# Second maxima and probabilities moved ahead of the output sum and its squares in a hybrid block's steady step

## The reference

```python
# group A, per chunk (the kernel takes tiles of 128 rows)
v_new = u_n - w_n @ state
o     = q_dec_n @ state + qk_n @ v_new
state = state * g_last_n + k_dec_n.T @ v_new
o_a   = rms_norm(o, gdn_norm_w) * silu(z)
# group B
probs = softmax(concat([scores, sink]))[..., :-1]
out   = probs @ vb
# both
mix = concat([o_a, o_b]) @ w_out
x   = x + rms_norm(mix, g_post_mix)
```

## Time and profile before

| | us |
|---|---|
| median of 3 runs | 1205.57 (1204.86 to 1207.25) |
| the profiled execution, its own time | 1205.73 |
| its span, first to last instruction | 1203.8 |
| PE busy | 1170.7 (97%) |
| PE weight loads busy | 990.8 (82%) |
| DVE busy | 807.1 (67%) |
| ACT busy | 540.3 (45%) |
| POOL busy | 383.0 (32%) |

### The profile page before, as it was taken

How to read it: one execution, slowest core, us unless ns; L and a number is a source line. 1 busy time by engine, 2 the same in 40 slices (tenths; PEclk the granted TensorE clock), 3 DMA queues, 4 the chain that set the end, 5 groups by cost and what they waited for, 6 DMA issues and landing times.

```text
span 1203.8 us, 17013 instructions
## 1 busy us (share of the span) xinstructions
PE 1170.7 (97%) x6014; PEld 990.8 (82%) x6014; DVE 807.1 (67%) x1148; ACT 540.3 (45%) x974; POOL 383.0 (32%) x345
## 2 busy tenths in 40 slices
PE   9999999998899999989899999999999999999997
PEld 8888888887798888877688888888888877888886
DVE  6432355467766677768987878778787777664557
ACT  6221153556355444436644444445444444643451
POOL 1222000211133322221266586556855551000001
PEclk9999999999899999999999999999999999999999
DMA  8321133546232333222145353544436467997613
GB/s 287 128 89 73 59 98 112 152 139 225 82 111 76 92 94 117 60 85 82 70 175 175 140 194 125 206 164 151 169 146 210 140 210 260 365 369 229 192 54 140
DMA packets 118296, 181.89 MB, mean 151 GB/s; under 512 B 20527, under 2 KB 78671, under 8 KB 113999
## 3 DMA queue, kind: packets, MB, share of 16 engines
q1 hardware_dynamic: 118223, 180.94, 44.4%
HBM read 123.21 MB, written 57.70 MB: 150 GB/s over the span
## 4 chain that ended last, share of the span: by engine, by line
PE 43%; DVE 5%; POOL 2%; issue 2%; DMA 1%; ACT 1%; SPq 0%; DVEq 0%; POOLq 0%; ACTq 0%
PE f_ps_up L3034 5%; PE f_ps_up L3036 5%; PE f_ps_up L3035 5%; PE sums L3034 5%; PE sums L3036 5%; PE sums L3035 5%; PE f_ps_up L3109 3%; PE f_ps_up L3111 3%; PE f_ps_up L3110 3%; PE sums L3111 2%; PE sums L3110 2%; PE sums L3109 2%; DMA stage<-in_w_down 1%; DVE f_conv L2754 1%; POOL conv L2993 1%
## 5 line engine op out<-in xcount | busy, mean ns | idle before, releaser
L2989 POOL TENSOR_TENSOR f_w_raw<-stage 128x512 f32<-128x512 f32 x40 | 65.5, 1639 | 109.6 <-PE f_ps_up L3036 108.8
L2719 DVE TENSOR_TENSOR f_w<-f_w_raw,f_w 128x512 fp32r<-128x512 f32 (+1 forms) x54 | 69.9, 1314 | 28.9 <-POOL f_w_raw L2989 28.9
L2993 POOL TENSOR_TENSOR conv<-conv 128x512 f32<-128x512 f32 x44 | 72.6, 1650 | 43.2 <-DMA conv<-in_w_down 40.6
L233 PE MATMUL sums<-split,slab_w 128*128 128x512 f32 x192 | 76.0, 396 | 0.5 <-PEq L284 0.5
L2993 POOL TENSOR_TENSOR f_conv<-f_conv 128x512 f32<-128x512 f32 x44 | 65.0, 1478 | 33.1 <-DMA y_blocks<-f_conv 29.8
L235 PE MATMUL sums<-split,slab_w 128*128 128x512 f32 x192 | 74.9, 390 | 0.0
L234 PE MATMUL sums<-split,slab_w 128*128 128x512 f32 x192 | 74.8, 390 | 0.0
L254 DVE SCALAR_TENSOR_TENSOR conv<-sums,conv_taps,conv 128x1023 f32<-128x1023 f32 (+6 forms) x39 | 46.7, 1199 | 37.3 <-ACT conv L245 36.4
L3034 PE MATMUL f_ps_up<-split,f_w 128*128 128x512 f32 x176 | 69.0, 392 | 2.8 <-PEq L812 1.4
L2519 ACT CAST f_w<-f_w_raw 128x512 fp32r<-128x512 f32 (+1 forms) x54 | 42.7, 790 | 58.5 <-POOL f_w_raw L2989 54.6
L3036 PE MATMUL f_ps_up<-split,f_w 128*128 128x512 f32 x176 | 68.6, 390 | 0.0
(11 more groups left out here) (444 smaller groups left out, 3465.8 us busy)
## 6 DMA issues: line engine op xcount, KB each, us to landing
stage<-in_w_up SPq DMA_DIRECT2D x22, 1024.0 KB, 5.4
y_blocks<-f_conv SPq DMA_DIRECT2D x22, 1024.0 KB, 5.0
conv<-in_w_down SPq DMA_DIRECT2D x11, 1024.0 KB, 7.3
w_down_sums<-conv SPq DMA_DIRECT2D x11, 1024.0 KB, 10.6
stage<-y_blocks SPq DMA_DIRECT2D x40, 256.0 KB, 5.7
f_rest_raw<-y_blocks SPq DMA_DIRECT2D x37, 256.0 KB, 5.6
x_tile<-in_x SPq DMA_DIRECT2D x12, 512.0 KB, 4.2
stage<-in_w_in SPq DMA_DIRECT2D x6, 1024.0 KB, 6.5
```

Of the source, the lines that this page charges most:

```text
L233: pe.matmul(bank, w_hi, h_hi[:, k, cols], start=(k == 0), stop=False)
L2719: dve.tensor_tensor(out, src, hi.bitcast(F32), ALU.subtract).then_inc(s_lo[name], 1)
L2989: pool.tensor_tensor(raw_sum(m), a, b, op).then_inc(s_add[m], 1)
L2993: pool.tensor_tensor(view(out), view(a), view(b), op).then_inc(signal, 1)
```

## The change

Four moves, all in `step`. On DVE, `a_mask(t, 6)` goes ahead of `a_bv`; `c_max(t + 1, 1)` goes from behind `a_qk` to a place between `b_state` and `b_o`. On ACT, `c_exp(t + 1, 1)` goes ahead of `b_square`, and ahead of the next tile's squares stands a wait of ACT for the count of its own `b_square`. The order of PE, POOL and SP is not changed, nor any operation.

```diff
@@ scalar, step @@
                 if b:
                     b_v_new(t, a)
-                    b_square(t)
                 if a:
                     c_exp(t + 1, 1)
+                if b:
+                    b_square(t)
                 if not a:
...
                 if a:
                     c_pt(t + 1, 1)
+                if b:
+                    after(act, o_sq, t)
                 if n:
                     a_square(t + 2, par)
@@ vector, step @@
                 if b:
+                    a_mask(t, 6)
                     a_bv(t, par)
-                    a_mask(t, 6)
                     b_resid(t, par)
...
                 if b:
                     b_state(t, par)
+                if a:
+                    c_max(t + 1, 1)
+                if b:
                     b_o(t)
                 if a:
                     a_qk(t + 1)
-                    c_max(t + 1, 1)
                 if b:
                     b_ms(t)
                     b_mix(t, par)
```

## The result

| | before | after |
|---|---|---|
| median of 20 runs each, us | 1204.84 (1204.17 to 1208.0) | 1208.47 (1205.27 to 1210.79) |
| ratio, 95% interval | | 1.0026 [1.0019, 1.0033] |
| mean granted clock, share of full | 0.9979, 0.9973, 0.9973 (the kernel before in the three groups of runs below) | 0.9956 (the 20 runs) |
| profiled execution, its own time, us | 1205.73 | 1206.6 |
| its span, us | 1203.8 | 1204.8 |

The account below looks back on a forecast made before the run. A closed loop DVE, ACT, PE, with PE 97% busy, was taken to bound the kernel. Steps 2 to 5 −0.8, step 6 −0.3, step 7 +0.15: −0.95 us against 1205.57, giving 1204.6 us; range 1202.2 to 1206.8.

Parts of the forecast that it names:

- Mask ahead of the values' product: DVE swap lets PE issue L2000 0.5 to 0.6 us earlier; 0.3 of it gets past the new values (L2028).
- the residual starts where it did: On DVE, swapping mask and values' product leaves the residual's start unchanged; the addition behind it moves by 0.1 at most.
- Maxima ahead of the output sum: On DVE, the second maximum starts at 402.15 in place of 403.35; its scores are done 0.6 us before.
- probabilities ahead of the squares: On ACT, exponentials start at 403.06, removing PE's 0.66 us wait at L2078; exponentials plus squares stay a 2.7 us block.
- what is late next: PE's sums of squares (L1910) wait 0.7 us for ACT's L1318; 0.2 us per step stays, bounds 0.05 and 0.3.
- The added wait o_sq: On ACT ahead of L1318, for squares already over: taken as 0, bounds 0 and 0.19 us.
- the norm chain: Output squares, GpSimd's power, DVE's L1672 come 1.6 us later; DVE's idle time ahead of L1550 used up, not exceeded.
- Step 1: No copy of a turned tile there; the exponentials start where they did: taken 0, bounds −0.1 and +0.3 us.
- Steps 6 and 7: Step 6: PE's product with the values comes forward, −0.3 us; step 7: residual and new values slip, +0.15 us.
- W: Theory from the experiments: mask first, the residual waits 0.2 us for DVE's fresh values' product, putting DVE's run 0.27 back.
- A: Rival: L1318 released earlier, both PE gaps close for good, 0.95 us per step, 1201.6 us; chance 0.12.
- B: Rival: slower, a later L1672 pushes L1550 and the next step's first addition; 1208.2 us at 1.5 later; chance 0.06.

Follow-up runs that it names:

- m1: Kernel before with only the last mask moved ahead of the values' product: 1206.53 us, ratio 1.0011 [0.9999, 1.0022].
- m2: Changed kernel with the mask back behind the values' product, so only maxima, probabilities and squares moved: 1206.76 us, ratio 1.0015 against the kernel before.
- m9: The changed kernel measured once more, unaltered, beside its filled version: 1209.34 us, ratio 1.0023 against the kernel before.
- m11: Changed kernel with two unread 128x512 products on PE ahead of the new values, steps 2 to 5: 1209.83 us, ratio 1.0028 against the kernel before.
- m12: Kernel before with seven unread 128x64 copies on ACT ahead of the next queries' squares, steps 2 to 5: 1213.68 us, ratio 1.0059.
- m6: Kernel before with three unread 128x128 copies on ACT ahead of the next queries' squares, steps 2 to 5: 1207.38 us, ratio 1.0012.
- m7: Changed kernel with the next queries' squares early on ACT and the old order of mask and values' product: 1201.59 us, ratio 0.9959 against the kernel before.
- m3: Changed kernel with the next queries' squares moved on ACT to right behind the new values: 1203.09 us, ratio 0.9982 against the kernel before.
- m5_fill: Changed kernel without the mask swap, plus three unread 128x512 products on PE ahead of the sums, steps 2 to 5: 1202.89 us, ratio 0.9976 against before.
- m10_after_fill: Changed kernel plus three unread 128x512 products on PE ahead of the sums of squares, steps 2 to 5: 1203.16 us, ratio 0.998 against the kernel before.
- m8: Changed kernel with the next queries' squares early and `d_ms` between the values' product and the residual: 1200.23 us, ratio 0.9947 against the kernel before.

## Why the prediction was wrong, point by point

**Mask ahead of the values' product: the failed step is "the residual starts where it did".** It starts 0.26 later, and the rows of tile t - 2, with the rest of DVE's run behind them, 0.28. I had read gaps of 0.2 us behind DVE's own results in this very trace and named them in the first part, and priced one where I thought of ACT; I did not ask whether the swap would make a new one. The first addition moved by 0.1, as said, but the gain of 0.3 past the new values did not come: they wait 0.42 to 0.46 for that addition (0.1 was forecast). Here the prediction's own rows allowed less than it took. It had the addition end at 391.65 + 0.1 = 391.75 and the new values before at 391.91, so at most 0.16 could be gained; and in after the new values start 0.15 behind the addition's end (389.77 against 389.21 + 0.41), which uses that up. m1 shows the part alone at +0.25 per step.

**Maxima ahead of the output sum, probabilities ahead of the squares, what is late next: right.** L2083 waits for nothing, L1318 did not move ahead in its step, and the sums wait 0.59 to 0.67 (0.7 was forecast), released by L1318:

```profile
401.27 0.37 ACT L1380 ACTIVATE m_probs<-m_ps_c,m_c_stat 128x128 f32<-128x128 f32 x1 [9.68 <-DVE m_c_stat L1685]
...
402.75 0.32 ACT L1360 ACTIVATE m_junk<-stage 128x128 bf16<-128x128 f32 x1
...
403.92 1.07 ACT L1418 COPY h_t<-sums 128x512 f32 x2
...
405.34 0.67 ACT L1318 ACTIVATE m_v_new<-m_qkv_odd 128x512 f32<-128x512 f32 x1
405.87 0.30 ACT L1324 ACTIVATE m_junk<-m_ps_a 128x128 bf16<-128x128 f32 x1
```

Block of exponentials and squares: 403.92 − 401.27 = 2.65, forecast 2.7. m2 shows this half at −0.17 per undisturbed step, forecast −0.2. The added wait o_sq and the norm chain cost nothing: L1672 comes 2.0 later, counted from the first maximum, where 1.6 was forecast, and DVE has no idle time left ahead of the norms of tile t + 2, but PE's turn behind the next step's first addition waits in none of the steps 2 to 5 of after.

**The new wait itself: a missing term.** I moved 0.6 us of idle time from one place on PE to another and priced it as equal. At L2078 it had been harmless to the clock; at the sums it is not. Each lowered stretch costs 37.06 − 35.55 = 1.5 us (1.53 to 1.56 in m2, m9, m11 and m12). No term for it stood in the sum, nor in the bounds of the new wait, nor among the rivals. The rule that the prediction weighed (the Trainium skill, Perfetto Trace Analysis, Optimization Strategy: find the gaps of the most contended engine and get what they wait for to start sooner) says nothing there of the clock behind a gap either. The Trainium skill (TensorE: Matmul & The Clock Gate, A second HAM failure mode: psum-queue depth-cycling) tells of a kernel in which PE is idle for short moments between groups of products so often that its clock goes back and forth between the two levels; here one wait of 0.47 to 0.68 us at this place was enough, in 11 steps. That page bore on the case, and was not weighed.

**Step 1: the row was read in a lowered stretch.** I took 0 (−0.1 to +0.3), because its scores began at 331.37, after the output sum at 331.33. It is −0.6 (36.07 against 36.62; 35.97 to 36.07 in every kernel with the probabilities first and no lowered stretch in that step, 36.65 to 36.74 in m1, m6 and m12). The scores of the earlier trace rows were late: in before, PE had run at 0.57 over the stretch 320 to 324. In mask alone, undisturbed there, they begin almost 1 us ahead of the output sum (330.86), and PE waits for the probabilities, which the change cures. A lowered stretch in this step costs nothing in the old order, where PE would have waited (36.65 and 36.74 in m6 and m12, with one, 36.68 in m1, without), and 1.1 us in the new one (37.16 in m7, with one). First the windows view of before, then PE of mask alone:

```profile
320.00:324.00 4.00, 3.91 (x21) 3.54 (x21) 3.79 (x11) 1.38 (x3) 0.00 (x0) 0.57 0.88 314
```

```profile
329.90 1.05 PE L2071 MATMUL m_ps_c<-m_k_b,m_q_b 128*128 128x128 f32 x8
334.52 0.66 PE L2078 MATMUL m_ps_c<-table,m_probs 128*128 128x128 f32 x4 [0.84 <-ACT m_probs L1380]
```

**Steps 6 and 7.** From `a_low` of step 6 to the feed-forward part: before 66.73, after 66.96. m2 alone gives −0.2 (forecast −0.3), m1 +0.36 (forecast +0.15, which had W left out here as well).

**The range.** Its lower end was added up wrongly: 0.3 per step, 0.3 in step 6, 0.1 in step 1 and nothing lost in step 7 give 1205.57 − 1.6 = 1204.0, not 1203.4. The miss is at the other end.

**Rivals.** A did not come, and its point of decision was the right one: where the squares are there early, the sums and the probabilities wait for nothing (m3, m7). That m7 measures the 1201.6 us that A had said is in part chance: it has the old order of mask and values and keeps its wait of 0.51 to 0.57 at the level's product, gains 0.80 per step where A had said 0.95, and 0.6 in step 1 where A had nothing. B, slower by the norm chain, did not occur; the kernel got slower by another mechanism. That B's figure of 1208.2 lies near the measured 1208.47 is chance.

**The sum of the two profiled executions closes**: 1.63 less ahead of step 1 (before has a lowered stretch in step 0 that after has not; the change doesn't reach there), 0.55 less in step 1, 1.92 more in steps 2 to 5, 0.23 more up to the feed-forward part, 1.1 more in that: +1.07, against spans that differ by 1.06. Against the medians, with the clock of all runs in place of the two profiles':

| us | step 1 | steps 2 to 5, undisturbed | steps 6, 7 | clock | feed-forward | sum | measured |
|---|---|---|---|---|---|---|---|
| after | −0.6 | +0.4 | +0.2 | +2.0 to 2.8 | +1.1 | +3.1 to 3.9 | +3.6 |
| m1_mask_only | 0 | +1.0 | +0.4 | −1.0 | +0.9 | +1.3 | +1.3 |
| m5_fill | −0.6 | −0.8 | −0.3 | −0.5 | −1.0 | −3.2 | −3.1 |
| m10_after_fill | −0.6 | +0.3 | +0.2 | −1.1 | −1.0 | −2.2 | −2.0 |

The clock is the difference of the mean clocks times 1205 us; feed-forward is read from one profile of each kernel, and steps 6 and 7 of m10, which hold a lowered stretch, are taken from after. The work of the change, in the sense of the prediction, comes to 0.0 (forecast −0.95); some 2 to 2.8 of the 3.6 us is the clock. This is an estimate and rather high: a stretch of 3.4 us at half clock loses 1.7 us of full-speed time and was seen to cost 1.5, which makes it 1.8 to 2.5.

**What stays open.** First, the column "feed-forward". The first 264 products of the down projection (from 986.9 in before) take 60.9 us in before, 62.0 in after and m8, 61.5 in m9, 59.8 to 59.9 in m5 and m10, though all run the same instructions there. PE's waits for splits of DVE come to 0.3 us there in before, 1.2 in after, 1.0 in m8 and m9, and none in m5 and m10. What holds the splits isn't shown: a DMA issue of SP takes 1.25 us in after where the same one takes 0.43 in m5, but issues of over 1 us stand in every profile, each time at other places. One profile of each doesn't tell cause from chance; so about 1 us of after's loss, and of the filled kernels' gain, is placed but not explained: that much of them may have nothing to do with the change. Second, why the wait lowers the clock in only about half of the steps: the same kernel had one lowered step in one profile and three in another (after, m9). Third, what in this place makes it: the length of the wait counts (0.2 did nothing, 0.47 and more did), but no run keeps the wait and changes the products around it.

## What to carry to other kernels

When a wait is moved on TensorE, look at what surrounds it in its new place, and read the granted clock beside every stretch, in the profile of before too: a row from a lowered stretch is no basis for a sum, and here a lowered stretch cost more than the wait that preceded it (1.5 against 0.6 us). A few products that nobody reads, put into that wait, are a cheap test and here even a gain; it is better to have what is waited for ready earlier, as with the early squares. When two instructions are swapped, see whether a reader now stands directly behind its writer on the same engine, and put a small instruction that reads neither between them.

## What the runs showed of the hardware that was not expected

- A wait of 0.43 to 0.68 us ahead of the sums of squares, on a TensorE that is 97% busy, is followed in 11 of 20 steps by about 3.4 us at the lower level, which begins 1.7 to 2.9 us behind the end of the wait and costs 1.5 us each. With 0.2 us at the same place: none of 4. With 0.89 to 0.98 at another place: none of 4.
- The changed kernel takes 1203.2 us with three unread products of 128x512 in that wait and 1209.3 without (clock 0.9982 against 0.9953); some 1.6 us of that lie in a part that the products don't reach.
- A vector instruction that reads what the one ahead of it has just written has 0.20 us of idle time ahead of it and starts 0.28 later than behind another one; through a small mean that GpSimd needs, the rest of DVE's run got the same 0.28 (steps longer by 0.25).
